# Start-up order of small transfers, and the place of layer 1's router fetch, in a two-layer encoder kernel with a mixture of experts

## The reference

```python
for i in range(DEPTH):                      # DEPTH = 2
    h = rmsnorm(x, ln_mix[i])               # norm weights of the mixer
    qkv = h @ w_qkv[i]
    q, k = rmsnorm(q, q_norm[i]), rmsnorm(k, k_norm[i])
    if i % N_MIXERS == 0:
        o = global_attention(rope(q), rope(k), v)
    else:
        o = window_attention(q, k, v, rel_bias, sinks[i // N_MIXERS])
    x = x + o @ w_o[i]
    x = x + hier_moe(rmsnorm(x, ln_ffn[i]), w_group[i], w_expert[i], w1[i], w3[i], w2[i])
# hier_moe: g = softmax(t @ w_group); e = t @ w_expert; best group, its two best experts;
#           y = sum over both of weight * (silu(t @ w1[e]) * (t @ w3[e])) @ w2[e]
```

## Time and profile before

| what | us |
|---|---|
| median of 3 runs | 635.72 (635.12 to 636.45) |
| span of the profiled execution, first to last instruction | 634.3 |
| TensorE busy | 620.9 (98%) |
| VectorE, ScalarE, GpSimd busy | 180.1, 139.3, 53.3 |
| mean DMA rate over the span | 362 GB/s |

### The profile page before, as it was taken

One profiled execution on the slowest core, in us unless ns is written; L12 is line 12 of the kernel. 1 busy time (PEld: TensorE's weight loads), 2 busy tenths in 40 slices (PEclk: granted clock), 3 DMA queues, 4 the chain that ended last, 5 costly groups with the idle time before them and its releaser, 6 DMA issues.

```text
span 634.3 us, 10484 instructions
## 1 busy us (share of the span) xinstructions
PE 620.9 (98%) x4409; PEld 255.9 (40%) x4409; DVE 180.1 (28%) x609; ACT 139.3 (22%) x372; POOL 53.3 (8%) x61
## 2 busy tenths in 40 slices
PE   8999999999999999999999999999999999999996
PEld 5445544434324334333244454453343343343221
DVE  1665834412102102100133667343111021021011
ACT  2136642210000000000131677331100000000011
POOL 0005420000000000000010475000000000000000
PEclk9999999999999999999999999999999999999999
DMA  8999909699999999999999997697999999999993
GB/s 318 293 270 421 385 3 368 228 418 420 422 421 420 422 422 419 421 420 420 399 295 243 346 405 272 239 380 268 421 419 421 421 421 421 421 420 421 419 418 122
DMA packets 44759, 229.94 MB, mean 362 GB/s; under 512 B 8271, under 2 KB 8561, under 8 KB 21666
## 3 DMA queue, kind: packets, MB, share of 16 engines
q1 hardware_dynamic: 43068, 224.66, 90.7%
q0 software_dynamic: 1312, 4.23, 2.0%
q10 hardware_dynamic: 326, 0.31, 0.2%
HBM read 228.10 MB, written 1.08 MB: 361 GB/s over the span
## 4 chain that ended last, share of the span: by engine, by line
PE 91%; DVE 3%; ACT 2%; DMA 2%; issue 1%; POOL 0%; DVEq 0%; ACTq 0%
PE ps L1462 35%; PE ps L1474 18%; PE ps L1220 12%; PE ps L1307 8%; PE ps L1400 5%; PE ps L1431 3%; PE ps L1289 2%; PE ps L1255 2%; PE ps L1276 1%; ACT attw L572 1%; PE ps L1538 1%; PE ps L1444 1%; DMA ring<-bias_rows 1%; DMA x_sb<-in_x_dram 1%; DVE attw L872 1%
## 5 line engine op out<-in xcount | busy, mean ns | idle before, releaser
L1462 PE MATMUL ps<-attw,work 128*32 128x512 f32 x1216 | 140.1, 593 | 0.0
L1474 PE MATMUL ps<-ring,work 128*32 128x512 f32 x960 | 105.0, 593 | 0.5 <-ACT work L651 0.5
L1462 PE MATMUL ps<-ring,work 128*32 128x512 f32 x832 | 100.5, 594 | 0.0
L1220 PE MATMUL ps<-attw,work 128*128 128x512 f32 x192 | 87.4, 598 | 0.1
L1462 PEld LDWEIGHTS ps<-attw,work 128*32 128x32 f32 x1216 | 40.1, 110 | 89.1 <-issue 89.1
L1307 PE MATMUL ps<-attw,work 128*128 128x512 f32 x128 | 60.0, 602 | 0.7 <-issue 0.5
L1474 PEld LDWEIGHTS ps<-ring,work 128*32 128x32 f32 x960 | 30.3, 110 | 70.0 <-issue 68.3
L1025 DVE TENSOR_TENSOR work<-work,ps 128x256 f32<-128x256 f32 (+1 forms) x24 | 11.5, 508 | 156.0 <-PE ps L1462 156.0
L1462 PEld LDWEIGHTS ps<-ring,work 128*32 128x32 f32 x832 | 27.3, 110 | 57.6 <-issue 52.7
L1220 PEld LDWEIGHTS ps<-attw,work 128*128 128x128 f32 x192 | 34.6, 190 | 37.9 <-issue 36.9
L440 POOL TENSOR_SCALAR attw<-attw,stat 128x256 f32<-128x256 f32 x40 | 40.8, 1024 | 51.8 <-DVE stat L886 51.6
(11 more groups left out here) (161 smaller groups left out, 459.9 us busy)
## 6 DMA issues: line engine op xcount, KB each, us to landing
ring<-in_w_dram SPq DMA_DIRECT2D x112, 1024.0 KB, 26.2
attw<-in_w_dram SPq DMA_DIRECT2D x80, 1024.0 KB, 20.2
attw<-in_w_qkv_dram SPq DMA_DIRECT2D x4, 2048.0 KB, 17.4
attw<-in_w_o_dram SPq DMA_DIRECT2D x8, 1024.0 KB, 22.9
attw<-in_w_qkv_dram SPq DMA_DIRECT2D x8, 512.0 KB, 11.0
ring<-bias_rows POOLq DMA_DIRECT2D x16, 256.0 KB, 7.2
x_sb<-in_x_dram SPq DMA_DIRECT2D x2, 512.0 KB, 7.0
out_dram<-x_sb SPq DMA_DIRECT2D x2, 512.0 KB, 4.5
```

The costliest lines, as they stand in the source:

```text
L1220: last = pe.matmul(ps[:, g, :], xT[:, k, P * tt:P * tt + P], wqkv[part][:, k, :], start=(k == 0), stop=(k == KB - 1))
L1462: last = pe.matmul(ps[row:row + SLOTS, bank[t], :], xg[:, k, t, row:row + SLOTS], w[:, e, k % 4, :], start=(k == 0), stop=(k == KB - 1), t ...
L1474: last = pe.matmul(ps[row:row + SLOTS, bank[t], :], hT[t][:, k, row:row + SLOTS], w[:, e, k % 2, 512 * half:512 * half + 512], start=(k == ...
```

## The change

Norm weights go first on ACT's queue, before the identity, and TensorE turns them before `x` tile 0. The rest of the table leaves ACT's queue and stands on SP's, behind `x` tile 1 and ahead of the small rows. Layer 1's router weights are issued after layer 0's last unit is used, ahead of layer 1's units 0, 1 and 2, and no longer behind unit 6; layer 0's stay where they were.

```diff
@@ SP
             sp.dma_start(x_sb[:, 1, :], xv[:, 1, :]).then_inc(x_landed[1], 16)
+            sp.dma_start(consts[:, P:TABLE], table[:, P:TABLE]).then_inc(table_landed, 16)
             sp.dma_start(ffn_rows, ln_ffn.rearrange("l (k p) -> (l k) p", p=P)).then_inc(rows_landed, 16)
...
                 load_held(L, 6)
-                load_router(L)
                 if L == 0:
+                    load_router(L)
                     sp.dma_start(next_gains[:, :, :], ...)
...
                 if L + 1 < DEPTH:
                     wait_used(L, LAST)
+                    load_router(L + 1)
                     load_held(L + 1, 0, 1, 2)
@@ ACT
+            act.dma_start(mix_rows, ln_mix.rearrange("l (k p) -> (l k) p", p=P)).then_inc(turn_landed, 16)
             act.dma_start(ident, table[:, 0:P]).then_inc(ident_landed, 16)
-            act.dma_start(mix_rows, ln_mix.rearrange("l (k p) -> (l k) p", p=P)).then_inc(turn_landed, 16)
...
-            act.dma_start(consts[:, P:TABLE], table[:, P:TABLE]).then_inc(table_landed, 16)
@@ TensorE
             pe.wait_ge(ident_landed, 16)
             ng = DEPTH * KB
-            turn_x(0, 0, [0])
             pe.wait_ge(turn_landed, 16)
             pe.transpose(ps[:, 0, 0:ng], mix_rows, ident[0:ng, 0:ng]).then_inc(gains_turned, 1)
+            turn_x(0, 0, [0])
             turn_x(0, 0, [1])
             stay_awake(2)
```

## The result

The changed kernel takes 638.87 us (median of 5, 637.4 to 638.93) against 635.72 us (5 runs, 635.12 to 636.45): ratio 1.004, 95% interval 1.0029 to 1.0051. It is slower, by more than the 0.2% that can be told apart, and it lies outside the range of the prediction. The five executions lie apart: two at 637.4 and 637.65 us, three at 638.87 to 638.93 us. The profiled one is the fastest, 637.4 us with a span of 635.5 us, so the profile shows only part of the median's loss. Its span has to be compared with the span of before (634.3): in later runs time and span of one execution lay 1.8 to 1.9 us apart, so the profiled execution of before took about 636.1 and not 635.7. The profiles thus differ by 1.2 us, the medians by 3.15.

What follows compares the result with a forecast made beforehand. The prediction took TensorE, 91% of the chain against DMA's 2%, to bound the kernel. Its terms, -0.02 - 0.10 + 0 + 0 = -0.12 us, took 635.72 to 635.6 us, no difference, with 634.9 to 636.4 for 8 in 10.

Steps and rivals of the forecast that it cites:

- What bounds the kernel: Whole kernel: TensorE holds 91% of the chain, DMA 2%; the change touches only the first 14 us and layer 1's attention.
- Start, norm weights: First 7.3 us: TensorE waits for the identity instead of `x`, projection begins at 7.32 against 7.34; -0.02, bounds -0.15 to +0.18.
- a start released by `x` near 5.4: Start: with the identity in by 5.2, the 0.16 hides in the wait for `x`; projection at 7.19, gain 0.15.
- Start, table: Start, weight load at 8.86: second k/v quarter lands earlier, its 0.40 us wait shrinks to 0.24; -0.10, bounds 0 and -0.16.
- The router's place, readers covered: Layer 1: router weights land ahead of their reader and expert units ahead of theirs, over 30 us of cover; zero.
- By order and bytes the queue ends where it ended, near 394.: Layer 1, SP's queue: ten unit DMAs land later by under 8 us, the queue's end stays near 394; no cost.
- rival D: Layer 1's expert weights come late, SP held at L318 longer and DMA engines running dry; 637 us or more, chance 0.02.
- The last bias tiles: Layer 1's attention, last two steps: tiles landing 6.9 us after issue stay about so; 0, bounds -0.2 and +1.2.
- rival A: Last score maxima, 391 and 393.8: last bias tile takes 8.1 instead of 6.9 us, path +1.2, 636.8 us; chance 0.12.
- a sign of being wrong: Layer 1's attention: the prediction is wrong if its length changes by over 1 us.
- The four tiles from 371 to 380: Layer 1's attention: bias tiles already beside large transfers took 7.2, 6.9, 7.2, 6.7, mean 7.0; so +0.1 at most, taken 0.
- Rival B: Last two bias tiles: router's pieces hold them up, so both waits, 0.97 and 0.93, vanish; 633.7 us, chance 0.08.

## Why the prediction was wrong

- **What bounds the kernel:** right. Everything outside the first 14 us and layer 1's attention kept its length.
- **Start, norm weights:** the mechanism was right (TensorE waits for the identity instead of `x`), the term was -0.02 with +0.18 as its bound and measured +0.12 in the profile, 7.46 for 7.34; other executions of the changed kernel began at 7.40 to 7.55. Only 0.05 of it is a later first piece (5.57 for 5.52); the turning of the norm weights took 0.28 us in place of 0.16, since TensorE was still at its slower pace. The bound of a start released by `x` near 5.4 was wrong: `x` lands at 3.9 to 4.2 in every kernel with the norm weights first. VectorE was not the limit, as said.
- **Start, table:** I counted -0.10. The wait vanished, but it had cost the chain nothing (6.25 for 6.24 us), so the term was 0. Together the start does not show in the times: 635.79 against 635.81.
- **The router's place, readers covered:** right. Neither the router nor any unit was late for its own reader.
- **The step that failed:** "By order and bytes the queue ends where it ended, near 394." It ended at 396.8, and with other contents. Before, the router's light pieces ended the queue at 394.3, 0.4 us behind unit 6, and left the engines a fifth idle from 386 to 394. After, they stand ahead of the units, the engines are half idle from 350 to 355, and the ten unit DMAs end 4.0 us later (391.2 for 387.2), unit 6 3.0 us later. Bytes were the wrong measure of the router's 2048 pieces: 80 KB are 0.2 us at the prediction's 0.40 MB/us. Its other bound for them, under 8 us, held, but with it the end near 394 does not follow. I had a dry stretch as part of rival D and gave it a price only for the units' readers, not for the tiles beside them.
- **The last bias tiles:** this is the term that followed from it. I took 0 and had +1.2 as the bound, rival A at 0.12. Rival A is what the profiles show: the last tile landed in 8.0 us and attention grew by 1.16, over the 1 us that I had named as a sign of being wrong. Its price of 636.8 does not reach the median of 638.87. The four tiles from 371 to 380 were the wrong witnesses. They had units beside them and took about 7.0 before and after alike; the last one takes 8.0 to 8.2 in five of the six profiled executions of the changed kernel and 9.0 where unit 6 is freshly issued beside it. Why the same neighbours cost 1 us more there is not settled.
- **Rival B** was right that the waits can vanish, and wrong in what holds the tiles up. With unit 6 late and the router where it was, its pieces are in the queue to 387.5 and the tile issued at 384.2 still lands in 4.0 us; with the pieces gone and unit 6 there it takes 6.6 us. So unit 6 is what counts. And it is worth 0.45 us and not 1.9, since another chain stands close behind.

The Trainium skill, DMA: Bandwidth & Descriptors, Queues, rings and completion order, says that an engine takes turns between queue rows, a packet at a time. The trace agrees: one of the last two tiles takes 3.7 to 4.8 us with little beside it and 6.1 to 9.0 with units beside it. The prediction had set this aside because of four tiles under units at 6.7 to 7.2; why tiles beside such units lie so far apart no run here shows.

What stays open: three of the five timed executions took 638.9 us, 1.5 us more than the profiled one, and none of the six profiles of the changed kernel shows such an execution. They belong to the router's move and unit 6: the router moved alone has three at 638.6 to 639.4, the start alone stays at or under 636.6, and so does the changed kernel with unit 6 late, twelve executions each. What the 1.5 us are made of is not shown. Two candidates of that size were seen, each in one profile of another kernel. One is the half clock behind a late tile, 1.6 us with the router behind the units. Worked out, 3.4 us at half clock lower the mean granted clock of an execution by 0.003. All five executions of that kernel have 0.995 to 0.997. So have the three of the router alone at 638.6 to 639.4, where its three shortest have 0.998 to 0.999. But of the changed kernel's three at 638.9 only one stands out: 0.998, 0.995 and 0.998, against 0.999 and 0.998 of the two others. The other candidate is a start at half pace to about 10 us, 1.7 us with the norm weights first alone; the router alone has before's start, and there no profile shows it.

## What to carry to other kernels

When a transfer is moved within a full queue, its own reader and the readers behind it are half of the account. The other half is what then passes at the old place, beside the small transfers of another queue that a stage waits for: ask which bytes travel while the last of them is in flight, and keep large prefetches out of that window if their reader has time. A wait in the trace is worth only its distance to the next chain, here 0.5 of 1.9 us when it is taken away. When it grows it can be worth more than its length: look at TensorE's granted clock behind it.

## What was not expected of the hardware

- Short pieces in a queue hold the issuing engine far longer than their bytes: 64 KB in 1024 pieces held SP for 15.3 to 24.1 us behind a full queue (L318), and for 10.1 and 10.8 us where unit 6 was late and the router's place as before. The next DMA behind them, of 1 MB, held it for another 6.3 us in the changed kernel.
- With such pieces at the head of SP's queue the DMA engines did not fill: a share of 0.51 to 0.57 and 82 to 104 GB/s from 350 to 355 in the nine profiles with the router ahead of the units on SP.
- The same 64 KB on ACT's queue, beside SP's full one, took 54.6 us to land.
- A 256 KB tile with 1 KB rows on POOL's queue landed in 3.7 us with little beside it and in 9.0 us beside 2 MB issued at the same time.
- Just behind 2.36 us without work TensorE ran at a granted clock of 0.50 for 3.4 us, and six matmuls took 3.77 us in place of 2.16. The moment at which TensorE reached its full pace in the start moved between about 4 and 10 us from one profile to another.
